# Seven column tiles of a projection taken in 512-column passes, their halves summed by ScalarE and VectorE, with two weight splits and one product moved

## The chip, the cores and the metric

The kernel runs on one NeuronCore of a Trainium2 chip. The metric is the device time of one execution in microseconds (us), the median of several runs.

The profile calls the engines PE (TensorE: matmuls; PEld is its weight load), DVE (VectorE), ACT (ScalarE), POOL (GpSimd) and SP (SyncE, which here only starts DMAs). A line such as L1335 is line 1335 of the kernel before.

## The reference

Three transformer blocks on one sequence of 256 tokens and 2048 features, all in float32. The first two (a pooling mixer and a dilated attention, each with an MLP) are not touched. The third block's mixer projects the normalised tokens once, and splits the result into four parts:

```python
hn = _rmsnorm(h, attn_norm_w[l])
proj = hn @ w_in[l]                       # 2048 -> 1024 + 512 + 256 + 64
u, c_q, c_kv, k_pe = jnp.split(proj, split_at, axis=-1)
y_ssm = _s5_group(u, ...)                 # a scan over the 256 tokens
y_mla = _mla_group(c_q, c_kv, k_pe, ...)  # 8 attention heads
```

`u` drives a diagonal state-space scan. `c_q` (512 columns) and `c_kv` (256) are each RMS-normalised and projected again to the queries, keys and values of eight heads. `k_pe` (64 columns) is a rotary key that all heads share.

## The kernel before

Every matmul weight is a float32 matrix that arrives from HBM in chunks of 128 x 2048 (1 MB; some are narrower). There are four slots. For each chunk SP starts the DMA into `raw` (L525), ACT rounds it into `whi` (`hi1`, L630), and DVE takes the difference `wlo = raw - whi` (`lo1`, L1335); the rounded type runs at full matmul rate. These two steps are called the split of a chunk. A slot of `raw` is loaded anew once its `lo1` is done, in the order of SP's queue; `whi` and `wlo` are free when PE has used the chunk (`chunk_used`). The tokens are held in the same two parts, side by side in `x_pair`: for each of 16 blocks of 128 features, 256 columns of `xhi` and 256 of `xlo`. A product is the sum of three matmuls, as `three` writes them:

```python
pe.matmul(o, w_hi, x_hi, start=first, stop=False)
pe.matmul(o, w_hi, x_lo, start=False, stop=False)
return pe.matmul(o, w_lo, x_hi, start=False, stop=last)
```

The chunks of the mixer have a fixed order, `MIXER`: 0 to 14 are the column tiles of the first projection (tiles 0 to 7 are `u`, 8 to 11 `c_q`, 12 and 13 `c_kv`, 14 `k_pe`), 15 is the value projection `v`, 16 to 18 are heads 0 to 2 (`mla`; 1280 columns wide for even heads, 768 for odd ones), 19 and 20 heads 3 and 4. Each engine works through a list written out by hand, in program order, and waits on counting semaphores.

PE's list in this stretch is: tiles 4 to 6; `drive` 0 and 1 (products that feed the scan of the first half of the state); tiles 7 to 9; `drive` 2 and 3; tiles 10 to 12; `read_out(0)`, which reads the scanned states of the first half; tiles 13 and 14; the sums of squares of the q norm and the kv norm (`norm`, a product with ones); `twin_k`, two products that give the rotary key in both of its forms; `read_out(1)`; and then the heads: `project_q(0)`, `project_v`, `project_k(0)`, `project_q(1)`, scores and so on. A tile of the projection (`proj_tile`, which calls `quad_tile`) takes 16 feature blocks with three matmuls of 256 columns each, and accumulates in one half of a PSUM bank; four tiles share two banks.

ACT's list: splits; `copy_u` (moves `u` out of PSUM); `copy_state` (the driven states); `copy_in(2)` (tiles 8 to 11, 1024 columns in one copy, into `mix_in`), `copy_in(3)` (tiles 12 to 14); the squares of the two norms; `y_copies`, which move the read-out of the first half in 16 pieces; the roots and roundings of the norms; from `copy_q` on the heads, with the v copies (`copy_v_all`) between pieces of the second read-out.

DVE's list: the `lo1` of each chunk between pieces of the scan. The scan of each half has `scan_steps` (`steps_of`), `scan_levels`, and `close_scan` (`scan_carry`, `scan_shift`, and the signal `scan_done`). DVE does 12 of 16 state pairs of a half, POOL the other 4 by a list of its own. After the second half come `wave_k` (multiplies the rotary key by its wave), the q norm, `lo1` of chunk 17, the kv norm, `rope_k` (copies the two products of `twin_k`), pieces of the second read-out, and the heads. `read_out(1)` waits for `scan_done` of the second half, `project_v` for `rope_k` and the kv norm, and the heads for the v copies.

Of the kernel before, what the change touches and what calls it, by code (L numbers as in the profile page):

```python
# [16 lines left out]
ALU = mybir.AluOpType  # L17
ACT = mybir.ActivationFunctionType
AX = mybir.AxisListType

P = 128
T = 256
D = 2048
DT = D // P
# [156 lines left out]
def build(nc, x_t, x_rows, gain_rows, weights, ssm_compact, ssm_skip, features, consts, dist_table, ssm_lam, positions, out):  # L181
    with ExitStack() as ctx:
        def sem(name):
            return ctx.enter_context(nc.semaphore(name))
# [137 lines left out]
        def half(bank, h):  # L322
            return ps[:, bank, h * T:(h + 1) * T]

        def block_ps(b):

            return ps[:, 2 * b:2 * b + 2, :].rearrange("p b (h t) -> p (b h) t", t=T)

        def wait_used(eng, q, s=SLOTS - 1):

            eng.wait_ge(chunk_used, q * SLOTS + (SLOTS + s + 1))
# [12 lines left out]
        def ccol(name, a=0, n=None, rows=P):  # L344
# [37 lines left out]
        angles_ready, trig_ready, table_ready = sem("angles_ready"), sem("trig_ready"), sem("table_ready")  # L382
        drive_done, state_copied, scan_done, scan_rest_done, y_done, y_ready = (
            sem(n) for n in ("drive_done", "state_copied", "scan_done", "scan_rest_done", "y_done", "y_ready"))
        x_tail_free, mla_sq, mla_var, mla_root = sem("x_tail_free"), sem("mla_sq"), sem("mla_var"), sem("mla_root")
        ssm_sq, ssm_var, ssm_root, ssm_high, ssm_low, y_other = (sem(n) for n in ("ssm_sq", "ssm_var", "ssm_root", "ssm_high", "ssm_low", "y_other"))
        gelu_ready, gelu_hi_ready, gelu_lo_ready, glu_sig, gated = (
# [4 lines left out]
                             "m_turned", "m_pt", "m_out", "m_out_copied"))  # L392
        act_steps, dve_steps, pool_steps = sem("act_steps"), sem("dve_steps"), sem("pool_steps")

        source = {"q": [(block_free, 2 + BLOCK["proj"] + 3)], "kv": [(block_free, 2 + BLOCK["proj"] + 4)]}

        def norm_tmp(name):

# [2 lines left out]
        def norm_ps(name):  # L401

            return half({"q": 0, "kv": 1}[name], 0)

        def down_ps(nb):

# [216 lines left out]
        def _(act):  # L623
# [19 lines left out]
            def norm_squares_ahead(name, src):  # L643

                for p in range(PIECES[NORM[name]]):
                    norm_square(name, src, p)

            def norm_root(name):
                k = NORM[name]
                act.wait_ge(norm_lo, LO0[name])  # L650
                act.wait_ge(norm_var, k + 1)
                act.activation(std[:], norm_ps(name), ACT.Sqrt, scale=1.0 / (NORMS[k][1] * P), bias=ccol("rms_eps")).then_inc(norm_std, 1)
# [411 lines left out]
            def hi_mixer(i0, i1):  # L1064
                for c in MIXER[i0:i1]:
                    hi_of(*c)
# [12 lines left out]
                        ins = act.activation(dst, src, ACT.Copy)  # L1079
                ins.then_inc(block_free, 1)  # L1080

            def copy_in(b):
                wait_used(act, *PLACE["proj", 4 * b + 3 if b < 3 else 14])
                n = 4 if b == 2 else 3
                act.activation(mix_in[:, 4 * b - 8:4 * b - 8 + n, :], block_ps(b % 2)[:, 0:n, :], ACT.Copy).then_inc(block_free, 1)

            def copy_state(i):

                act.wait_ge(drive_done, i + 1)
                act.activation(state[:, :, 4 * i:4 * i + 4, ROUND:], ps[:, 4 + i % 4, :].rearrange("p (e r c) -> p r e c", e=4, r=2),  # L1090
                               ACT.Copy).then_inc(state_copied, 1)
# [21 lines left out]
            hi_mixer(12, 14)  # L1113
            for i in range(4, 8):
                copy_state(i)
            hi_mixer(14, 16)
            copy_in(2)
            hi_mixer(16, 18)
            act.wait_ge(x_tail_free, 1)
            y_copies(0, 0, 4, False)  # L1120
            act.wait_ge(x_tail_free, 2)
            norm_squares_ahead("q", mix_in[:, 0:4, :])
            copy_in(3)
            norm_squares_ahead("kv", mix_in[:, 4:6, :])
            norm_root("q")
            hi_mixer(18, 19)
            y_copies(0, 4, 6, False)
# [201 lines left out]
        def _(dve):  # L1329
# [18 lines left out]
            def norm(name, gain, src, dst_hi, dst_lo):  # L1348
                k = NORM[name]
                n, t0 = NORMS[k][1], PIECE0[k]  # L1350
                w = min(4, n)
                y = norm_tmp(name)
                dve.wait_ge(norm_std, k + 1)
                step(dve.reciprocal(rstd[:], std[:]))
                step.settle()

                def lo(p):
                    dve.wait_ge(norm_hi, LO0[name] + p + 1)
                    a = slice(p * w, p * w + w)
                    dve.tensor_tensor(dst_lo[:, a, :], y[:, a, :], dst_hi[:, a, :].bitcast(F32), ALU.subtract).then_inc(norm_lo, 1)  # L1360
                for p in range(PIECES[k]):
                    for i in range(p * w, p * w + w):
                        ins = dve.scalar_tensor_tensor(out=y[:, i, :], in0=src[:, i, :], scalar=fcol(gain, i),
                                                       in1=rstd[:], op0=ALU.mult, op1=ALU.mult)
                    ins.then_inc(norm_y, 1)
                    if p >= 1:
                        lo(p - 1)
                lo(PIECES[k] - 1)
# [608 lines left out]
            def lo_mixer(i0, i1):  # L1977
                for c in MIXER[i0:i1]:
                    lo1(*PLACE[c], mixer_width(*c))

            def steps_of(hf, j0, j1):
                scan_steps(dve, step, scan_tmp, 16 * hf, SCAN_DVE, j0, j1)

            def close_scan(hf):
                for s0 in range(0, SCAN_DVE, 6):
                    scan_carry(dve, step, scan_tmp, 16 * hf + s0, 6)
                scan_shift(dve, step, 16 * hf, SCAN_DVE)
                dve.sem_inc(scan_done, 1)

            def wave_k():  # L1990

                dve.wait_ge(trig_ready, 5)
                dve.wait_ge(block_free, 2 + BLOCK["proj"] + 4)
                dve.tensor_tensor(k_waved[:], mix_in[:, 6, :], rope_wave[:], ALU.mult).then_inc(k_wave_ready, 1)
# [80 lines left out]
            scan_levels(dve, step, scan_tmp, 0, SCAN_DVE)  # L2075
            lo_mixer(12, 13)
            close_scan(0)
            lo_mixer(13, 14)
            dve.wait_ge(state_copied, 7)
            steps_of(1, 1, 3)  # L2080
            lo_mixer(14, 15)
            steps_of(1, 3, 6)
            lo_mixer(15, 16)
            steps_of(1, 6, 8)
            lo_mixer(16, 17)
            scan_levels(dve, step, scan_tmp, 16, SCAN_DVE)
            close_scan(1)
            wave_k()
            norm("q", "mla_q_norm_w_2", mix_in[:, 0:4, :], cq_hi, cq_lo)
            lo_mixer(17, 18)  # L2090
            norm("kv", "mla_kv_norm_w_2", mix_in[:, 4:6, :], ckv_hi, ckv_lo)
            rope_k()
            dve.wait_ge(y_done, 2)
# [317 lines left out]
        def _(pe):  # L2411
# [5 lines left out]
            def chunk(q, s):  # L2417
                pe.wait_ge(lo_ready, q * SLOTS + (SLOTS + s + 1))
# [102 lines left out]
            def quad_tile(q, set_, s, slot, n_used, x_ready=None, order=range(DT), free=False):  # L2521

                chunk(q, slot)
                o = block_ps(set_)[:, s, :]
                for n, k in enumerate(order):
                    if x_ready is not None and n % 4 == 0:
                        pe.wait_ge(x_ready[0], x_ready[1] + n // 4 + 1)
                    c = slice(k * P, k * P + P)
                    ins = three(o, whi[:, s, c], wlo[:, s, c], xhi[:, k, :], xlo[:, k, :], n == 0, n == DT - 1)
                    if free and n in (3, 7):  # L2530
                        ins.then_inc(x_tail_free, 1)
                ins.then_inc(chunk_used, n_used)

            def norm(name, src):
                k = NORM[name]
                n, t0 = NORMS[k][1], PIECE0[k]
                w = min(4, n)
                for p in range(PIECES[k]):
                    pe.wait_ge(norm_sq, t0 + p + 1)
                    for i in range(p * w, p * w + w):  # L2540
                        ins = pe.matmul(norm_ps(name), ones[:], norm_tmp(name)[:, i, :], start=i == 0, stop=i == n - 1)
                ins.then_inc(norm_var, 1)
# [356 lines left out]
            def proj_tile(i):  # L2899
                if i % 4 == 0:  # L2900
                    pe.wait_ge(block_free, n0 + i // 4 + 1)
                q, s = PLACE["proj", i]
                if i == 14:
                    quad_tile(q, i // 4 % 2, i % 4, s, 1, order=LAST_ORDER, free=True)
                else:
                    quad_tile(q, i // 4 % 2, i % 4, s, 1)
            rows_mixed("attn2", QUAD["mixer"], 512, turn_mixer)
            pe.wait_ge(rows_staged, 1)
            proj_tile(4)
# [2 lines left out]
                proj_tile(i)  # L2912
            drive(0)
            drive(1)
            for i in range(7, 10):
                proj_tile(i)
            drive(2)
            drive(3)
            for i in range(10, 13):
                proj_tile(i)  # L2920
            read_out(0)
            for i in range(13, 15):
                proj_tile(i)
            norm("q", mix_in)
            norm("kv", mix_in)
            twin_k()
            read_out(1)

            def project_q(h):

# [329 lines left out]
```

## Time and profile before

| | |
|---|---|
| median of 3 runs | 3127.41 us (3127.34 to 3127.64) |
| profiled execution | 3128.01 us, span 3126.2 us |
| busy share of the span | PE 99%, PEld 83%, DVE 65%, ACT 63%, POOL 14% |
| the stretch from the projection's tile 4 to the first heads | about 2129 to 2262 us of the span |

The span runs from the first to the last instruction of the profile. A busy share is an average over many stages with different limits, and matmuls overlap their neighbours, so PE's 99% is not its peak. Times of rows are counted from the start of the span. In a timeline the start of a matmul is the moment of its issue; the distance from one start to the next is what a matmul costs in a stream, and its own duration, which is longer, is not.

### The profile page before, as it was taken

Reading aid. Unit: us, or ns where it says so; the run is one execution under the profiler, and the core shown is the slowest. Engines: PE = TensorE matmul, PEld = TensorE weight load, DVE = VectorE, ACT = ScalarE, POOL = GpSimd, SP = SyncE. Lnnn points to the kernel's source line nnn. Section 1 sums busy time; section 2 is a strip of 40 time slices with the busy share of each in tenths; the row PEclk is TensorE's granted clock in tenths of the full one; section 3 lists DMA queues with packets and bytes.
Section 4 is the critical chain, followed back from the end, with each engine's and each line's share of the span. In section 5 each row is a group of like instructions: output and inputs, shape, how many; then the busy total and the mean of one; then the engine's idle time right before and its main releaser. Section 6 shows DMA issues by size and latency. Waiting matters only on the chain.

```text
span 3126.2 us, 40499 instructions
## 1 busy us (share of the span) xinstructions
PE 3104.1 (99%) x14653; PEld 2605.3 (83%) x14653; DVE 2032.4 (65%) x1815; ACT 1971.1 (63%) x2737; POOL 447.3 (14%) x562
## 2 busy tenths in 40 slices
PE   9999999999999999999999999999999999999998
PEld 8888888888888888888888888879988888888887
DVE  6876665566565554667655656576876676666767
ACT  7557677666766776666555455556655866666655
POOL 3112443344352000000000000003330000000000
PEclk9999999999999999999999999999999999999999
DMA  8555665565556544546555555536454555545553
GB/s 312 192 201 214 214 211 204 204 218 210 197 174 230 194 176 162 188 162 263 194 189 187 201 190 199 187 136 239 148 190 181 200 190 204 196 175 201 188 203 119
DMA packets 114035, 612.91 MB, mean 196 GB/s; under 512 B 11040, under 2 KB 39840, under 8 KB 43936
## 3 DMA queue, kind: packets, MB, share of 16 engines
q1 hardware_dynamic: 91360, 597.10, 52.1%
q10 hardware_dynamic: 22592, 14.69, 1.5%
q8 instruction: 55, 0.90, 0.1%
q14 instruction: 28, 0.23, 0.0%
HBM read 599.16 MB, written 12.58 MB: 196 GB/s over the span
## 4 chain that ended last, share of the span: by engine, by line
PE 96%; DVE 2%; ACT 1%; issue 0%; DMA 0%; ACTq 0%; DVEq 0%
PE ps L2550 28%; PE ps L2552 28%; PE ps L2551 28%; PE ps L2421 1%; PE ps L2422 1%; PE ps L2423 1%; PE ps L2458 1%; PE ps L2451 1%; PE ps L2445 1%; DVE wlo L1335 1%; PE ps L2623 0%; PE ps L2875 0%; PE ps L2575 0%; PE ps L2777 0%; PE ps L2757 0%; ACT whi L630 0%
## 5 line engine op out<-in xcount | busy, mean ns | idle before, releaser
L1335 DVE TENSOR_TENSOR wlo<-raw,whi 128x2048 fp32r<-128x2048 f32 (+1 forms) x544 | 1245.6, 2300 | 786.1 <-ACT whi L630 782.8
L630 ACT ACTIVATE whi<-raw 128x2048 fp32r<-128x2048 f32 (+1 forms) x544 | 1025.4, 1901 | 853.0 <-PE ps L2552 787.8
L2550 PE MATMUL ps<-whi,x_pair 128*128 128x512 f32 x2400 | 935.9, 390 | 0.0
L2552 PE MATMUL ps<-whi,x_pair 128*128 128x512 f32 x2400 | 933.9, 389 | 0.0
L2551 PE MATMUL ps<-wlo,x_pair 128*128 128x512 f32 x2400 | 933.8, 389 | 0.0
L2552 PEld LDWEIGHTS ps<-whi,x_pair 128*128 128x128 f32 x2400 | 450.5, 188 | 93.8
L2551 PEld LDWEIGHTS ps<-wlo,x_pair 128*128 128x128 f32 x2400 | 450.6, 188 | 93.3
L2550 PEld LDWEIGHTS ps<-whi,x_pair 128*128 128x128 f32 x2400 | 450.6, 188 | 93.1
L2550 PE MATMUL ps<-whi,hid_hi 128*128 128x512 f32 x1280 | 499.3, 390 | 0.0
L2551 PE MATMUL ps<-wlo,hid_hi 128*128 128x512 f32 x1280 | 498.0, 389 | 0.0
L2552 PE MATMUL ps<-whi,hid_lo 128*128 128x512 f32 x1280 | 498.0, 389 | 0.0
L2552 PEld LDWEIGHTS ps<-whi,hid_lo 128*128 128x128 f32 x1280 | 240.3, 188 | 49.9
L2550 PEld LDWEIGHTS ps<-whi,hid_hi 128*128 128x128 f32 x1280 | 240.4, 188 | 49.8 <-issue 0.4
L2551 PEld LDWEIGHTS ps<-wlo,hid_hi 128*128 128x128 f32 x1280 | 240.4, 188 | 49.3
L1373 DVE TENSOR_TENSOR resid<-resid,ps 128x1024 f32<-128x1024 f32 x165 | 200.7, 1217 | 105.3 <-PE ps L2552 104.9
L702 ACT ACTIVATE hid<-up_turns 32x256 f32<-32x256 f32 x512 | 213.0, 416 | 6.1 <-DVE up_turns L1509 0.5
L452 POOL TENSOR_TENSOR scan_room<-state,hop 128x64 f32<-128x64 f32 (+3 forms) x20 | 10.0, 500 | 1199.2 <-ACT state L1090 1197.7
L2178 DVE SCALAR_TENSOR_TENSOR conv<-up_sum,feat,conv 128x255 f32<-128x255 f32 (+1 forms) x176 | 73.3, 479 | 85.7 <-ACT conv L1278 83.0
L927 ACT ACTIVATE qk_t<-qk_turns 32x256 f32<-32x256 f32 x192 | 80.0, 417 | 48.5 <-DVE qk_turns L1840 46.4
L2335 POOL TENSOR_TENSOR job_tmp<-compact,z_pow 128x128 f32<-128x128 f32 x32 | 70.9, 2215 | 85.2 <-DVEq L1783 82.3
L702 ACT ACTIVATE up_sum<-value_turns 32x256 f32<-32x256 f32 x176 | 73.4, 417 | 5.4 <-DVE value_turns L1509 3.5
L759 ACT ACTIVATE drive_out<-drive_turns 32x128 f32<-32x128 f32 x240 | 74.3, 310 | 3.0
(410 smaller groups left out, 3096.2 us busy)
## 6 DMA issues: line engine op xcount, KB each, us to landing
raw<-weights SPq DMA_DIRECT2D x536, 1024.0 KB, 4.8
read_tab<-read_tables SPq DMA_DIRECT2D x2, 3072.0 KB, 11.5
read_tables<-c_wide ACTq DMA_DIRECT2D x32, 128.0 KB, 1.9
drive_tables<-drive_out ACTq DMA_DIRECT2D x16, 256.0 KB, 3.7
drive_tab<-drive_tables SPq DMA_DIRECT2D x4, 1024.0 KB, 9.5
raw<-weights SPq DMA_DIRECT2D x6, 512.0 KB, 9.7
raw<-weights SPq DMA_DIRECT2D x4, 640.0 KB, 12.1
resid<-x_rows SPq DMA_DIRECT2D x1, 2048.0 KB, 13.0
```

Of the source, the lines that this page charges most:

```text
L630: act.activation(whi[:, s, 0:width], raw[:, s, 0:width], ACT.Copy).then_inc(hi_ready, 1)
L702: ins = act.activation(to, src, func)
L759: ins = act.activation(drive_out[32 * k:32 * k + 32, :, :, 32 * i:32 * i + 32].rearrange("p e r c -> p (e r) c"), drive_turns[32 * i:32 * ...
L927: ins = act.activation(to, part, ACT.Copy)
L1335: dve.tensor_tensor(wlo[:, s, 0:width], raw[:, s, 0:width], whi[:, s, 0:width].bitcast(F32), ALU.subtract).then_inc(lo_ready, 1)
L1373: return dve.tensor_tensor(r, r, ps[:, bank:bank + 2, :], ALU.add).then_inc(sem_, n)
L2178: ins = dve.scalar_tensor_tensor(out=o, in0=up_sum[:, half_, nt, 0:T - lag], scalar=fcol("ffn_conv_w_2", i + tap * (2 * FF2 // P)), in1=o, ...
L2335: step(pool.tensor_tensor(a, src.unsqueeze(2).to_broadcast(shape), straight, ALU.mult))
L2421: pe.matmul(o, w_hi, x_hi, start=first, stop=False)
L2550: pe.matmul(o, xh[:, k, t], whi[:, s, c], start=first and j == 0, stop=False)
L2551: pe.matmul(o, xh[:, k, t], wlo[:, s, c], start=False, stop=False)
L2552: ins = pe.matmul(o, xl[:, k, t], whi[:, s, c], start=False, stop=last and j == 3)
```

## The change

The seven tiles 8 to 14 are taken by a new function, `pair_tile`. For each feature block it has two matmuls instead of three: `whi` with the whole of `x_pair`, 512 columns, which fills a whole bank (high product in the first half, `whi` times `xlo` in the second), and `wlo` with `xhi`, 256 columns, accumulated in the first half. Each tile has a bank to itself: tiles 8 to 11 banks 0 to 3, tile 12 bank 0, tile 13 bank 2, tile 14 bank 3.

The two halves are summed by two engines: ACT copies the first half to `mix_in` (`copy_pair`, seven copies instead of two), and DVE adds the second half from PSUM to it (`pair_sum`). DVE's seven additions stand between the pieces of the scan; that of tile 13 stands ahead of `scan_levels` of the second half, that of tile 14 ahead of `wave_k`. DVE's splits (`lo1`) of chunks 15 and 16 move from between the `steps_of` of the second half to behind `wave_k` and behind the q norm. PE's `twin_k` moves from ahead of `read_out(1)` to behind it. Other waits follow the new banks.

```diff
@@ -382,6 +382,7 @@
         angles_ready, trig_ready, table_ready = sem("angles_ready"), sem("trig_ready"), sem("table_ready")
         drive_done, state_copied, scan_done, scan_rest_done, y_done, y_ready = (
             sem(n) for n in ("drive_done", "state_copied", "scan_done", "scan_rest_done", "y_done", "y_ready"))
+        pair_copied, pair_summed = sem("pair_copied"), sem("pair_summed")
         x_tail_free, mla_sq, mla_var, mla_root = sem("x_tail_free"), sem("mla_sq"), sem("mla_var"), sem("mla_root")
         ssm_sq, ssm_var, ssm_root, ssm_high, ssm_low, y_other = (sem(n) for n in ("ssm_sq", "ssm_var", "ssm_root", "ssm_high", "ssm_low", "y_other"))
         gelu_ready, gelu_hi_ready, gelu_lo_ready, glu_sig, gated = (
@@ -392,7 +393,7 @@
                              "m_turned", "m_pt", "m_out", "m_out_copied"))
         act_steps, dve_steps, pool_steps = sem("act_steps"), sem("dve_steps"), sem("pool_steps")
 
-        source = {"q": [(block_free, 2 + BLOCK["proj"] + 3)], "kv": [(block_free, 2 + BLOCK["proj"] + 4)]}
+        source = {"q": [(block_free, 2 + BLOCK["proj"] + 3)], "kv": [(pair_summed, 5)]}
 
         def norm_tmp(name):
 
@@ -401,6 +402,10 @@
         def norm_ps(name):
 
             return half({"q": 0, "kv": 1}[name], 0)
+
+        def pair_bank(i):
+
+            return {12: 0, 13: 2, 14: 3}.get(i, i % 4)
 
         def down_ps(nb):
 
@@ -1079,10 +1084,10 @@
                         ins = act.activation(dst, src, ACT.Copy)
                 ins.then_inc(block_free, 1)
 
-            def copy_in(b):
-                wait_used(act, *PLACE["proj", 4 * b + 3 if b < 3 else 14])
-                n = 4 if b == 2 else 3
-                act.activation(mix_in[:, 4 * b - 8:4 * b - 8 + n, :], block_ps(b % 2)[:, 0:n, :], ACT.Copy).then_inc(block_free, 1)
+            def copy_pair(i):
+
+                wait_used(act, *PLACE["proj", i])
+                act.activation(mix_in[:, i - 8, :], half(pair_bank(i), 0), ACT.Copy).then_inc(pair_copied, 1)
 
             def copy_state(i):
 
@@ -1113,15 +1118,18 @@
             hi_mixer(12, 14)
             for i in range(4, 8):
                 copy_state(i)
+            for i in range(8, 12):
+                copy_pair(i)
             hi_mixer(14, 16)
-            copy_in(2)
+            copy_pair(12)
             hi_mixer(16, 18)
+            copy_pair(13)
             act.wait_ge(x_tail_free, 1)
             y_copies(0, 0, 4, False)
             act.wait_ge(x_tail_free, 2)
             norm_squares_ahead("q", mix_in[:, 0:4, :])
-            copy_in(3)
             norm_squares_ahead("kv", mix_in[:, 4:6, :])
+            copy_pair(14)
             norm_root("q")
             hi_mixer(18, 19)
             y_copies(0, 4, 6, False)
@@ -1987,6 +1995,12 @@
                 scan_shift(dve, step, 16 * hf, SCAN_DVE)
                 dve.sem_inc(scan_done, 1)
 
+            def pair_sum(i):
+
+                dve.wait_ge(pair_copied, i - 7)
+                y = mix_in[:, i - 8, :]
+                dve.tensor_tensor(y, y, half(pair_bank(i), 1), ALU.add).then_inc(block_free if i in (11, 14) else pair_summed, 1)
+
             def wave_k():
 
                 dve.wait_ge(trig_ready, 5)
@@ -2075,19 +2089,25 @@
             scan_levels(dve, step, scan_tmp, 0, SCAN_DVE)
             lo_mixer(12, 13)
             close_scan(0)
+            pair_sum(8)
+            pair_sum(9)
             lo_mixer(13, 14)
             dve.wait_ge(state_copied, 7)
             steps_of(1, 1, 3)
             lo_mixer(14, 15)
+            pair_sum(10)
+            pair_sum(11)
             steps_of(1, 3, 6)
-            lo_mixer(15, 16)
+            pair_sum(12)
             steps_of(1, 6, 8)
-            lo_mixer(16, 17)
+            pair_sum(13)
             scan_levels(dve, step, scan_tmp, 16, SCAN_DVE)
             close_scan(1)
+            pair_sum(14)
             wave_k()
+            lo_mixer(15, 16)
             norm("q", "mla_q_norm_w_2", mix_in[:, 0:4, :], cq_hi, cq_lo)
-            lo_mixer(17, 18)
+            lo_mixer(16, 18)
             norm("kv", "mla_kv_norm_w_2", mix_in[:, 4:6, :], ckv_hi, ckv_lo)
             rope_k()
             dve.wait_ge(y_done, 2)
@@ -2531,6 +2551,25 @@
                         ins.then_inc(x_tail_free, 1)
                 ins.then_inc(chunk_used, n_used)
 
+            def pair_tile(i, order=range(DT)):
+
+                q, s = PLACE["proj", i]
+                if i == 14:
+                    pe.wait_ge(block_free, BLOCK["proj"] + 5)
+                elif i >= 12:
+                    pe.wait_ge(pair_summed, 2 * i - 23)
+                else:
+                    pe.wait_ge(block_free, BLOCK["proj"] + (3 if i < 10 else 4))
+                chunk(q, s)
+                bank, r = pair_bank(i), i % 4
+                for n, k in enumerate(order):
+                    c = slice(k * P, k * P + P)
+                    pe.matmul(ps[:, bank, :], whi[:, r, c], x_pair[:, k].rearrange("p h t -> p (h t)"), start=n == 0, stop=False)
+                    ins = pe.matmul(half(bank, 0), wlo[:, r, c], xhi[:, k, :], start=False, stop=n == DT - 1)
+                    if i == 14 and n in (3, 7):
+                        ins.then_inc(x_tail_free, 1)
+                ins.then_inc(chunk_used, 1)
+
             def norm(name, src):
                 k = NORM[name]
                 n, t0 = NORMS[k][1], PIECE0[k]
@@ -2900,10 +2939,7 @@
                 if i % 4 == 0:
                     pe.wait_ge(block_free, n0 + i // 4 + 1)
                 q, s = PLACE["proj", i]
-                if i == 14:
-                    quad_tile(q, i // 4 % 2, i % 4, s, 1, order=LAST_ORDER, free=True)
-                else:
-                    quad_tile(q, i // 4 % 2, i % 4, s, 1)
+                quad_tile(q, i // 4 % 2, i % 4, s, 1)
             rows_mixed("attn2", QUAD["mixer"], 512, turn_mixer)
             pe.wait_ge(rows_staged, 1)
             proj_tile(4)
@@ -2912,19 +2948,21 @@
                 proj_tile(i)
             drive(0)
             drive(1)
-            for i in range(7, 10):
-                proj_tile(i)
+            proj_tile(7)
+            for i in range(8, 10):
+                pair_tile(i)
             drive(2)
             drive(3)
             for i in range(10, 13):
-                proj_tile(i)
+                pair_tile(i)
             read_out(0)
-            for i in range(13, 15):
-                proj_tile(i)
+            pair_tile(13)
+            pair_tile(14, LAST_ORDER)
+            pe.wait_ge(pair_summed, 4)
             norm("q", mix_in)
             norm("kv", mix_in)
+            read_out(1)
             twin_k()
-            read_out(1)
 
             def project_q(h):
```

## Rows read from the trace of the kernel before

**Rows 1.** The page's chain of work that ended last, by engine.
```profile
PE 96%; DVE 2%; ACT 1%; issue 0%; DMA 0%; ACTq 0%; DVEq 0%
```

**Rows 2.** PE's waits, 2125 to 2420 us: total, times, longest.
```profile
PE ps L2550 <- DVE ssm_lo L2041: 0.9, 1, 0.9
```

**Rows 3.** PE's timeline: start, us, instruction, count [idle before <-releaser]; matmuls of two widths.
```profile
2127.59 1.98 PE L2498 MATMUL ps<-wlo,x_pair 128*128 128x512 f32 x8
2129.40 0.28 PE L2421 MATMUL ps<-x_pair,whi 128*128 128x256 f32 x1
2129.52 0.28 PE L2422 MATMUL ps<-x_pair,whi 128*128 128x256 f32 x1
```

**Rows 4.** PE's timeline, the first rows of five blocks.
```profile
2196.38 0.33 PE L2888 MATMUL ps<-u_step,read_tab 128*128 128x64 f32 x2
...
2207.02 0.36 PE L2421 MATMUL ps<-x_pair,whi 128*128 128x256 f32 x1
...
2221.30 0.59 PE L2896 MATMUL ps<-k_waved,const 128*128 128x256 f32 x2
...
2222.17 0.33 PE L2888 MATMUL ps<-u_step,read_tab 128*128 128x64 f32 x2
...
2235.76 0.40 PE L2960 MATMUL ps<-whi,ckv_hi 128*128 128x512 f32 x1
```

**Rows 5.** ACT's timeline, 2213 to 2242 us.
```profile
2213.11 0.85 ACT L630 ACTIVATE whi<-raw 128x768 fp32r<-128x768 f32 x1 [15.20 <-PE ps L2423]
...
2230.60 0.63 ACT L661 ACTIVATE ckv_hi<-kv_tmp 128x512 fp32r<-128x512 f32 x1
...
2235.96 0.39 ACT L1138 ACTIVATE m_io<-ps 128x256 f32<-128x256 f32 x1 [0.44 <-PE ps L2423]
...
2237.34 0.60 ACT L1149 ACTIVATE v_all<-ps 128x512 f32<-128x512 f32 x1 [0.31 <-PE ps L2962]
...
2241.42 0.60 ACT L1149 ACTIVATE v_all<-ps 128x512 f32<-128x512 f32 x1 [0.18 <-PE ps L2962]
```

**Rows 6.** DVE's timeline, 2200 to 2233 us.
```profile
2200.16 2.29 DVE L1335 TENSOR_TENSOR wlo<-raw,whi 128x2048 fp32r<-128x2048 f32 x1
...
2205.50 1.49 DVE L1335 TENSOR_TENSOR wlo<-raw,whi 128x1280 fp32r<-128x1280 f32 x1
2206.91 0.37 DVE L452 TENSOR_TENSOR scan_room<-state,hop 128x168 f32<-128x168 f32 x1
...
2211.51 0.61 DVE L483 TENSOR_TENSOR scan_room<-pow_re,state 128x294 f32<-128x294 f32 x1
...
2216.00 0.47 DVE L483 TENSOR_TENSOR scan_room<-pow_re,state 128x294 f32<-128x294 f32 x1
...
2219.79 0.22 DVE L498 COPY state<-state 128x168 f32<-128x168 f32 x1
...
2220.22 0.43 DVE L1994 TENSOR_TENSOR k_waved<-mix_in,rope_wave 128x256 f32<-128x256 f32 x1 [0.21 <-DVE state L498]
2221.10 1.75 DVE L1354 RECIPROCAL rstd<-std 128x256 f32<-128x256 f32 x1 [0.46 <-ACT std L652]
...
2227.70 1.75 DVE L1354 RECIPROCAL rstd<-std 128x256 f32<-128x256 f32 x1
2229.48 0.88 DVE L1363 SCALAR_TENSOR_TENSOR kv_tmp<-mix_in,feat,rstd 128x256 f32<-128x256 f32 x2
...
2231.87 0.68 DVE L1999 COPY k_rope<-ps 128x512 f32<-128x512 f32 x1
```

**Rows 7.** POOL's timeline, the last row of its scan.
```profile
2215.75 0.30 POOL L498 COPY state<-state 128x56 f32<-128x56 f32 x1
```

**Rows 8.** The page's DMA issues: count, KB each, us to landing.
```profile
raw<-weights SPq DMA_DIRECT2D x4, 640.0 KB, 12.1
```

**Rows 9.** Windows: us, busy of PE, PEld, DVE, ACT, POOL; PEclk, DMA share, GB/s.
```profile
111.00:114.30 3.30, 0.33 (x3) 0.14 (x3) 3.21 (x5) 0.05 (x1) 1.81 (x4) 1.00 0.59 199
114.90:118.30 3.40, 3.40 (x19) 3.40 (x18) 2.38 (x2) 2.21 (x2) 0.00 (x0) 0.50 0.59 248
```

## The prediction

> **What bounds the kernel now.** I read the page first, for the bound. The chain of work that ended last is 96% TensorE (PE); VectorE (DVE) and ScalarE (ACT) hold 3% [rows 1]. Whatever shortens PE's own work shortens the end, and whatever makes PE wait lengthens it. The change touches one stretch, so I next read PE's waits over 2125 to 2420 us, from the first projection tile to the output products: the longest entry is 0.9 us [rows 2]. There is hardly a wait here to win back. Then I read PE's timeline for the price of a matmul and the order of the blocks, ACT's and DVE's timelines for who has slack, POOL's for what runs beside DVE, and the granted clock.
>
> PE's order in the stretch is a chain without a hole: the first read-out from 2196.38, tiles 13 and 14 from 2207.02, the norm sums, the twin product from 2221.30, the second read-out from 2222.17, then the q product, the v product from 2235.76 [rows 4]. The second read-out needs DVE's scan, behind whose last piece `wave_k` starts at 2220.22 [rows 6]: about 2 us before PE arrives. That is all the slack that the scan has.
>
> **The matmuls.** Eight matmuls of 512 columns take from 2127.59 to 2129.40, 0.226 each; one of 256 columns is followed by the next after 0.12 [rows 3]. A tile is now 16 x 3 x 0.12 = 5.76 us and becomes 16 x (0.226 + 0.12) = 5.54. Seven tiles: PE saves 7 x 0.22 = 1.5 us, 0.05% of the time. That is the whole direct gain. No row alternates the two widths inside one bank. Where the width changes at 2129.40, nothing is added [rows 3], so I take 0.346 a step; as the other end a step keeps its 0.36 and the 1.5 us are not gained.
>
> The Trainium skill ("TensorE: Matmul & The Clock Gate", Back-to-back issue gap) gives a matmul its columns at the clock and a fixed 2.5 ns more; by that, dropping one matmul in three saves 16 x 7 x 2.5 ns = 0.3 us, an estimate. The rows show a larger part that does not grow with the columns (2 x 0.12 - 0.226 = 14 ns), and they decide.
>
> **The sums.** Before, two ACT copies took seven column blocks; now seven copies of 256 columns at 0.39 (the `m_io` copy from PSUM has that shape) [rows 5], and DVE gets seven additions of 128x256 with one operand in PSUM. No row has that form: 128x256 without PSUM is 0.43, a 128x512 copy from PSUM 0.68 [rows 6]. I take 0.43, whose shape is the same; the end above adds 0.25 to each, the end below is ACT's 0.39. The ACT copies themselves cost nothing: ACT stands idle 15.2 us before 2213.11 [rows 5]. The copy of tile 11 now stands ahead of the split of chunk 14 and holds it until tile 11 is done, near 2190; DVE comes to that chunk near 2194 and PE near 2212, so it is covered. Tiles 12, 13 and 14 wait for the sums of tiles 8, 10 and 11 to free their banks. By the same steps these end near 2188, 2197 and 2197, and the tiles begin near 2189.5, 2206 and 2211: covered, the first by 1.5 us, and a later sum would cost what it exceeds that by.
>
> **The new wait, and where it stands.** DVE works in program order. The sum of tile 13 stands before `scan_levels` of the second half, so the last part of the scan is queued behind tile 13. And PE runs tile 13 only after the first read-out. Before, ACT's split of chunk 17, released by the end of tile 13, starts at 2213.11 [rows 5]. Six tiles (8 to 13) are 0.22 shorter each: 2211.8. ACT first does that split (0.85), then the copy (0.39): 2213.05. With the sum: 2213.5. DVE gets there earlier: it began the split of chunk 16 at 2205.50; without the split of chunk 15 (2.29) [rows 6] and with five sums (2.15) that is 2205.4. So DVE stands idle some 7.7 us, with the rest of the scan, `wave_k`, both norms and the rope behind it.
>
> From 2206.91 (levels) to 2220.22 (`wave_k`) DVE needs 13.3 us [rows 6]. POOL ran its share beside it until 2216.05 [rows 7]. Of the sixteen carry operations the first eight took 4.49 (2211.51 to 2216.00), the next eight 3.79 (to 2219.79) [rows 6]. POOL does not wait for tile 13, and while DVE idles it has no company; it should be done when DVE resumes. So I take the later rate for all: levels 4.60 x 3.79 / 4.49 = 3.9, carry 7.6, rest 0.4, together 11.9 (bound above: the old 13.3; below: 11.2, if the levels gain twice as much). `wave_k` or what stands in its place comes at 2225.4 instead of 2220.22, and the scan's signal some 0.2 before. PE, with 1.5 us saved and the twin product (0.87) moved behind, arrives near 2222.17 - 2.4 = 2219.8 and waits 5.4 us.
>
> **What is late next.** The reciprocal of the q norm began at 2221.10. Now the sum of tile 14 (0.43), `wave_k` (0.43) and the moved split of chunk 15 (2.29) come first: 2228.5. The q norm and chunk 17's split take 6.6 (to 2227.70), chunk 16's moved split 1.4 (2205.50 to 2206.91): 2236.5, where the trace has 2227.70 [rows 6]. DVE is 8.8 us late, and with it the kv norm, `rope_k` (ends 2241.35 instead of 2231.87 + 0.68) and the copies behind it.
>
> PE's side of this: 2225.2, the read-out 10.6 (as 2196.38 to 2207.02), the twin products 0.9, the q product 3.0 (from 2232.8 to 2235.76) [rows 4]: 2239.7. Then it waits for the rope until 2241.35. Moving the twin product therefore costs nothing: DVE covers it by 1.6 us. Without that cover it would cost its own 0.9.
>
> ACT took `ckv_hi` at 2230.60; its input was there at 2229.48 + 0.88 = 2230.36 [rows 5, 6], but ACT was still copying. Now ACT waits for it until 2239.15, so ACT is 8.55 late. It gets back its three waits for PE that follow, 0.44 + 0.31 + 0.18 [rows 5], since the v product is only 5.6 us late. The last v copy, for which PE waits, is 8.55 - 0.93 = 7.6 us late. From there heads, softmax and the glu products pass from ACT to DVE to PE, with PE's holes under 1 us each [rows 2], so nothing gives the 7.6 us back.
>
> The moved splits issue no DMA, but free their raw slots 26 and 29 us later, and SP's queue, in order, holds chunks 19, 20 and all after them until then. Chunk 19 is asked for at 2228.5, chunk 20 near 2235.6; 640 KB take 12.1 us to land (median) [rows 8], so they are in by 2247.7. ACT turns to chunk 19 only after the last v copy (2241.42 + 0.60 [rows 5], now + 7.6: 2249.6). Hidden, by 2 us for the later chunk at the least; without that cover ACT would wait for the difference.
>
> **The sum.** PE's saved 1.5 us is spent inside the wait. Profiled execution 3128.0 (span 3126.2 and 1.8 around it) + 7.6 = 3135.6; the median of the runs is 0.6 under that execution, so 3135.0. With the scan at 13.3 it is 3136.4, with dearer sums on the path (13 and 14) 3136.9, with no gain on the tiles 1.3 more, 3138.2; with the scan at 11.2, 3134.3. About 0.2%, 6.3 us, can be told from no change here.
>
> **The clock.** After the one hole like the new one, 3 us at 111 us, the granted clock is 0.50, the lower level (1.2 GHz), for 3.4 us [rows 9]. A hole of 5.4 us should do the same in the read-out: up to 1.7 us lost there, twice that if two such stretches follow. PE has 1.6 us to spare at the rope, and its v products are 2 us ahead of ACT's copies, so I count nothing. The Trainium skill has it so too ("TensorE: Matmul & The Clock Gate", Why this matters for your kernels): a longer pause of PE between bursts puts the array at half clock. Here the trace agrees, 0.50 at 114.9 us; if none of it were hidden the sum would be 1.7 us more.
>
> **The rivals.** First, the loss is partly absorbed (no change by 0.2%): the scan alone on DVE, or the copies after it, run 1.4 us or more quicker than I sum, or ACT catches up in its gaps. For it: the margin over 6.3 us is only 1.3. Against it: PE's holes after 2240 are too small to take up a delay. About 3132.5. Second, on the other side, the wait does not bind: the sum of tile 13 is ready when DVE arrives at 2205.4. It decides from a sum done by about 2207. Then the scan ends by 2219, PE does not stall, chunk 16's 1.4 us and the sums lengthen the norm chain, and the 1.5 us from PE pays for them: 3127 to 3129. Against it: 10.6 us of read-out stand between tiles 12 and 13 [rows 4]. No row gives more than 1.5 us, so a gain over 0.2% needs an error elsewhere. Third, it is worse: the clock's loss is not hidden, or alternating the widths costs; 0.04 us a step more over six tiles is 3.8 us, all on the path: 3137.5 to 3140.
>
> **Chances.** As summed, 3133.8 to 3137.5: 0.6. Absorbed: 0.2. Wait not binding: 0.07. Worse: 0.13. The range 3130.0 to 3138.5 leaves out the second rival and the end of the third. Slower: 0.73; same 0.25; faster 0.02.
>
> **What would show it.** Right: DVE idle 7 to 8 us before the sum of tile 13, released by ACT; PE idle about 5 us at the first matmul of the second read-out, released by DVE; `rope_k` near 2241 and the v product behind it; tiles of 5.5 us; a clock row of 0.50 near 2226. Wrong: PE without a hole there, tiles other than 5.5 us, or PE's later blocks shifted by clearly less than the v copies.

## The result, and the profile after

The changed kernel takes 3144.45 us (median of 6 runs, 3143.48 to 3144.84), the kernel before 3127.91 beside it (6 runs): a ratio of 1.0053, 95% interval 1.0042 to 1.0063. It is slower by 16.5 us; the forecast was slower by 7.6, and the result lies above its range. The profiled execution is 3144.51 us, its span 3142.7.

The page's chain of work that ended last, by engine, is what it was [rows 1]:

```profile
PE 96%; DVE 2%; ACT 1%; issue 0%; DMA 0%; ACTq 0%; DVEq 0%
```

The page's shares don't show a loss of 0.5%. The view of PE's waits, 2125 to 2440 us (total, times, longest), does; its second row is the old longest one [rows 2]:

```profile
PE ps L2927 <- issue: 5.0, 1, 5.0
PE ps L2589 <- DVE ssm_lo L2055: 0.9, 1, 0.9
```

PE's timeline (start, us, instruction, count, idle before): first a piece of a pair tile, then the blocks [rows 3, 4]:

```profile
2160.71 0.40 PE L2567 MATMUL ps<-x_pair,whi 128*128 128x512 f32 x1
2160.94 0.28 PE L2568 MATMUL ps<-x_pair,wlo 128*128 128x256 f32 x1
2161.06 0.40 PE L2567 MATMUL ps<-x_pair,whi 128*128 128x512 f32 x1
...
2225.86 0.66 PE L2927 MATMUL ps<-u_step,read_tab 128*128 128x64 f32 x2 [4.96 <-issue]
...
2246.36 1.17 PE L2935 MATMUL ps<-k_waved,const 128*128 128x256 f32 x2
...
2247.82 0.78 PE L2441 MATMUL ps<-cq_hi,whi 128*128 128x256 f32 x1
...
2251.43 0.40 PE L2998 MATMUL ps<-whi,ckv_hi 128*128 128x512 f32 x1
```

The hole is there, 4.96 us, ahead of the second read-out. The row names no releaser; DVE's scan ends at 2225.70, 0.16 us before the read-out starts. But the read-out then lasts from 2225.86 to the twin product at 2246.36, 20.5 us where the first one took 10.6 [rows 4]. The v product starts 15.67 us later than before (2251.43 against 2235.76), and the hole is a third of that. The two executions do not reach the stretch at the same time, though. PE's first row of `drive` 0, which stands ahead of all that the change touches, in the kernel before and in the changed one:

```profile
2147.54 7.26 PE L2875 MATMUL ps<-u_step,drive_tab 128*128 128x64 f32 x64
2147.81 7.26 PE L2914 MATMUL ps<-u_step,drive_tab 128*128 128x64 f32 x64
```

So 0.27 us of that are none of the change's; counted from this row, the v product is 15.4 us late. Below, "from the drive" means counted in this way.

The windows (us, busy of PE, PEld, DVE, ACT, POOL; granted clock, DMA share, GB/s) say why [rows 9]:

```profile
2220.00:2226.00 6.00, 1.04 (x6) 0.61 (x5) 5.51 (x15) 2.85 (x4) 0.00 (x0) 0.93 0.00 0
2226.00:2230.00 4.00, 4.00 (x20) 4.00 (x20) 3.90 (x4) 0.00 (x0) 0.00 (x0) 0.50 0.01 2
2230.00:2240.00 10.00, 10.00 (x49) 10.00 (x48) 8.37 (x11) 6.26 (x10) 0.00 (x0) 0.50 0.36 115
2240.00:2249.00 9.00, 9.00 (x39) 8.64 (x39) 1.27 (x2) 4.41 (x6) 0.00 (x0) 0.50 0.26 107
2249.00:2260.00 11.00, 11.00 (x70) 9.84 (x69) 10.62 (x26) 7.54 (x18) 0.00 (x0) 1.00 0.00 1
```

The mean of 0.93 in the first row means that the clock fell to its lower level (0.50, 1.2 GHz) about 0.8 us before 2226, while PE stood. It came back only at 2249: 23.9 us, in the last 23.2 of which PE never stood. After the old hole it was low for 3.4 us [rows 9]. There, in the kernel before, products of 256 columns follow the hole:

```profile
114.31 0.35 PE L2421 MATMUL ps<-pool_hi,whi 128*128 128x256 f32 x1 [2.99 <-issue]
```

DVE's timeline (start, us, instruction, idle before and its releaser) [rows 6]:

```profile
2213.97 0.42 DVE L2002 TENSOR_TENSOR mix_in<-mix_in,ps 128x256 f32<-128x256 f32 x1 [8.93 <-ACT mix_in L1090]
2214.31 0.33 DVE L457 TENSOR_TENSOR scan_room<-state,hop 128x168 f32<-128x168 f32 x1
...
2225.48 0.22 DVE L503 COPY state<-state 128x168 f32<-128x168 f32 x1
...
2228.92 1.75 DVE L1362 RECIPROCAL rstd<-std 128x256 f32<-128x256 f32 x1
...
2236.91 1.75 DVE L1362 RECIPROCAL rstd<-std 128x256 f32<-128x256 f32 x1
...
2248.42 0.69 DVE L2013 COPY k_rope<-ps 128x512 f32<-128x512 f32 x1 [7.46 <-PE ps L2936]
```

The sum of tile 13 waits 8.93 us, and the scan and both norms follow it as forecast. The last row is not as forecast: DVE is ready for the rope at 2240.95 and waits 7.46 us for PE, where PE should have waited for DVE.

ACT's timeline, the copies behind the slow read-out and the last v copy [rows 5]:

```profile
2251.63 0.38 ACT L1146 ACTIVATE m_io<-ps 128x256 f32<-128x256 f32 x1 [7.14 <-PE ps L2443]
...
2257.10 0.60 ACT L1157 ACTIVATE v_all<-ps 128x512 f32<-128x512 f32 x1 [0.19 <-PE ps L3000]
```

The last v copy, for which the heads wait, is 15.68 us late (2241.42 before), 15.4 from the drive. From there on the delay stays what it is: the last rows of DVE's output are 15.6 us late as well. The other 0.9 of the 16.5 us by which the span is longer lie behind these rows: the span ends 5.8 us after they begin, and 4.9 before.

### The profile page after: what moved, and what is told of

It is laid out like the page before. It is cut to its first block, busy times and chain, and to the rows that moved or that the text cites. A ratio compares the mean times of both kernels' runs of the same rounds, so it can differ in the third digit from the quotient of the medians.

```text
span 3142.7 us, 40293 instructions
## 1 busy us (share of the span) xinstructions
PE 3116.0 (99%) x14541; PEld 2611.1 (83%) x14541; DVE 2033.2 (65%) x1822; ACT 1967.5 (63%) x2742; POOL 440.8 (14%) x562
## 4 chain that ended last, share of the span: by engine, by line
PE 96%; DVE 2%; ACT 1%; issue 0%; DMA 0%; ACTq 0%; DVEq 0%
PE ps L2589 28%; PE ps L2591 28%; PE ps L2590 28%; PE ps L2478 1%; PE ps L2567 1%; PE ps L2441 1%; PE ps L2471 1%; PE ps L2442 1%; PE ps L2443 1%; PE ps L2465 1%; DVE wlo L1343 1%; PE ps L2662 0%; PE ps L2914 0%; PE ps L2568 0%; PE ps L2614 0%
```

## The experiments

Theory A: the wait for tile 13 makes the scan late, PE gets a hole, and the hole costs twice, once as delay and once through a clock that stays low over the whole read-out. B: the read-out is slow by itself, from the new tiles or banks. C: the moved splits of chunks 15 and 16 make the norms late, and that is the loss. Ratios are to the kernel before on the same chip, with 95% intervals.

**The wait taken away.** The sum of tile 13 moves into the middle of the scan, which then doesn't wait for tile 13; all else is the changed kernel.

```diff
-            pair_sum(13)
             scan_levels(dve, step, scan_tmp, 16, SCAN_DVE)
-            close_scan(1)
+            scan_carry(dve, step, scan_tmp, 16, 6)
+            pair_sum(13)
+            scan_carry(dve, step, scan_tmp, 22, 6)
+            scan_shift(dve, step, 16, SCAN_DVE)
+            dve.sem_inc(scan_done, 1)
```

> Undoes the new wait alone: the sum of tile 13 stands between the two halves of scan_carry instead of ahead of scan_levels; all else is the changed kernel. Theory A (DVE's wait for tile 13 makes a hole of 5 us on PE, and the hole lowers the clock for the read-out): no wait of DVE over 1 us, scan done by about 2219, no hole, the read-out in 10.6 us, 3127 to 3129 us. Rival B (the read-out is slow because of something that the paired tiles bring): still 20 us for the read-out, 3137 or more. Rival C (the splits moved behind the scan make the norms late): about 3.7 us of the loss stay, 3131 to 3132.

Measured: 3129.16 us, ratio 1.0004 (0.9995 to 1.0013). Its window over most of the read-out, its DVE timeline, PE's rows (the drive, the read-out's start, the twin product behind it, the v product), and ACT's last v copy:

```profile
2222.00:2233.00 11.00, 11.00 (x95) 10.90 (x95) 9.11 (x14) 7.80 (x12) 0.00 (x0) 1.00 0.43 152
```

```profile
2212.53 0.42 DVE L2002 TENSOR_TENSOR mix_in<-mix_in,ps 128x256 f32<-128x256 f32 x1
...
2216.64 0.22 DVE L503 COPY state<-state 128x168 f32<-128x168 f32 x1
...
2232.34 0.68 DVE L2013 COPY k_rope<-ps 128x512 f32<-128x512 f32 x1
```

```profile
2146.36 7.26 PE L2917 MATMUL ps<-u_step,drive_tab 128*128 128x64 f32 x64
...
2219.28 0.33 PE L2930 MATMUL ps<-u_step,read_tab 128*128 128x64 f32 x2
...
2229.95 0.65 PE L2938 MATMUL ps<-k_waved,const 128*128 128x256 f32 x2
...
2233.73 0.40 PE L3001 MATMUL ps<-whi,ckv_hi 128*128 128x512 f32 x1
```

```profile
2241.05 0.60 ACT L1157 ACTIVATE v_all<-ps 128x512 f32<-128x512 f32 x1
```

No idle time before the sum, the scan done at 2216.9, no hole, the clock at 1.00, the read-out done in 10.7 us. The pair tiles and the moved splits are all in it, so neither B nor C holds. It gains nothing either: from the drive, its v product starts 0.85 us earlier than before, but the last v copy is 0.8 us later.

**The hole filled.** The changed kernel, with 22 products of 512 columns (chunk 15's rounded weights with themselves) while PE would stand, into a bank that the read-out overwrites afterwards; the late scan stays.

```diff
+            def dense(n):
+
+                q, s = PLACE["v", 0]
+                pe.wait_ge(hi_ready, q * SLOTS + (s + 1))
+                for _ in range(n):
+                    pe.matmul(ps[:, 7, :], whi[:, s, 0:P], whi[:, s, 0:512], start=True, stop=True)
...
             norm("kv", mix_in)
+            dense(22)
             read_out(1)
```

> The changed kernel, with 22 products of 512 columns added on PE between the kv norm and the second read-out (chunk 15 with itself, into a bank that the read-out then overwrites; they take 5.0 us and their result is not used). They fill the hole; DVE's wait for tile 13 stays. Theory A: clock 1.00 throughout, the read-out in 10.6 instead of 20.5 us, rope_k near 2241, and only the loss of the late scan is left: 3135 to 3137. Rival B: the read-out still takes about 20 us, 3144 to 3145.

Measured: 3136.69 us, ratio 1.0027 (1.0016 to 1.0037). PE's waits, its drive, and ACT's last v copy:

```profile
PE ps L2441 <- ACT v_all L1157: 2.0, 1, 2.0
PE ps L3006 <- DVE k_rope L2013: 1.2, 1, 1.2
```

```profile
2147.02 7.25 PE L2914 MATMUL ps<-u_step,drive_tab 128*128 128x64 f32 x64
```

```profile
2248.71 0.60 ACT L1157 ACTIVATE v_all<-ps 128x512 f32<-128x512 f32 x1
```

The clock stays at 1.00 and the read-out takes 10.7 us. Now PE waits for the rope, as forecast for the change itself. The last v copy is at 2248.71, from the drive 7.8 us later than before: that is the late scan alone. In the changed kernel it is 7.6 us later still: that is the clock.

**The wait alone.** The kernel before, with one line more and nothing else of the change.

```diff
             lo_mixer(16, 17)
+            wait_used(dve, *PLACE["proj", 13])
             scan_levels(dve, step, scan_tmp, 16, SCAN_DVE)
```

> The kernel before with one wait added: DVE waits for the end of tile 13 ahead of scan_levels of the second half. No paired tiles, no sums, no moved splits, no moved twin product. Theory A: scan done near 2225, a hole of 4 to 5 us on PE ahead of the twin product, the clock at 0.50 through the read-out, 3141 to 3144. Rival B: the hole costs its own length and the read-out keeps 10.6 us, 3132 to 3134.

Measured: 3144.78 us, ratio 1.0054 (1.004 to 1.0067), just above what A expected. PE's timeline and a window:

```profile
2226.11 1.22 PE L2897 MATMUL ps<-k_waved,const 128*128 128x256 f32 x2 [4.03 <-DVE k_waved L1994]
```

```profile
2226.00:2249.00 23.00, 22.89 (x103) 22.54 (x104) 9.71 (x15) 10.65 (x15) 0.00 (x0) 0.50 0.13 46
```

This one wait alone costs as much as the whole change, and the change without it costs nothing that can be told. Here the two twin products, 256 columns wide, still stand ahead of the read-out; they did not raise the clock, which stayed low for 27.3 us, to 2253.2.

**The splits back in their places.** The changed kernel with the splits of chunks 15 and 16 between the scan's steps again.

```diff
             pair_sum(12)
+            lo_mixer(15, 16)
             steps_of(1, 6, 8)
+            lo_mixer(16, 17)
             pair_sum(13)
...
             wave_k()
-            lo_mixer(15, 16)
             norm("q", ...)
-            lo_mixer(16, 18)
+            lo_mixer(17, 18)
```

> The changed kernel with the splits of chunks 15 and 16 back at their old places, ahead of the sum of tile 13, in DVE's idle time. Theory A: DVE stands ready 7.5 us before the twin product ends, so what it saves (3.7 us) is on no path: 3144 to 3145, as the changed kernel. Rival C: the moved splits are part of the loss, 3140 to 3141.

Measured: 3144.73 us, ratio 1.0054 (1.004 to 1.0068); a hole of 5.1 us, the clock low for 23.9 us. The norms come earlier, and DVE only waits longer for PE ahead of the rope: 10.90 us instead of 7.46. C is out.

**What follows the hole.** The hole stays, and 16 useless products (`dense`, as above) of 512 columns stand behind it, ahead of the read-out. Theory A2: what PE runs behind the hole decides how long the clock stays low. Theory D: it stays low for its time, whatever PE runs.

```diff
             norm("kv", mix_in)
+            pe.wait_ge(scan_done, 2)
+            dense(16)
             read_out(1)
```

> The changed kernel with the hole kept: PE waits for the scan as before, then does 16 products of 512 columns (chunk 15 with itself, result not used), then the read-out. Theory A2 (what comes after the hole decides how long the clock stays low: the read-out's products of 64 columns do not bring it back, products of 256 or 512 columns do): the 16 products take 4 to 7 us, part of them at 0.43 each, the clock returns during them, the read-out takes 10.6 us: 3139 to 3141. Rival D (the clock stays low for some 24 us whatever is done): 6.8 us for the products and 20 for the read-out, 3150 to 3152.

Measured: 3139.13 us, ratio 1.0036 (1.0024 to 1.0049). PE's timeline and three windows:

```profile
2224.59 6.33 PE L2943 MATMUL ps<-whi 128*128 128x512 f32 x16 [4.92 <-DVEq L1996]
2230.75 0.33 PE L2927 MATMUL ps<-u_step,read_tab 128*128 128x64 f32 x2
```

```profile
2225.00:2229.00 4.00, 4.00 (x10) 3.05 (x10) 3.90 (x4) 0.00 (x0) 0.00 (x0) 0.50 0.04 11
2229.00:2231.00 2.00, 2.00 (x10) 1.66 (x9) 1.97 (x5) 0.00 (x0) 0.00 (x0) 0.81 0.57 175
2234.00:2242.00 8.00, 8.00 (x71) 7.95 (x71) 5.00 (x6) 6.68 (x11) 0.00 (x0) 1.00 0.59 209
```

The same hole (its releaser, L1996, is the line that signals `scan_done`), and the clock is low for only 6.8 us: by the mean of 0.81 in the second window it is back near 2229.8, while the wide products run. The read-out then runs at full rate, 2230.75 to 2241.4. Six us of useless work on the path make the changed kernel 5.3 us faster. A2 holds, D does not. What it is in these products that raised the clock is not shown: they differ from the read-out's passes in width, in the number format (rounded weights, against plain float32 in two passes) and, from the two twin products of the wait alone, also in how long they run.

**Half of the hole filled.** 11 dense products ahead of the read-out instead of 22, so that 2.45 us of hole remain.

```diff
             norm("kv", mix_in)
+            dense(11)
             read_out(1)
```

> The changed kernel with 11 instead of 22 products of 512 columns ahead of the wait for the scan: a hole of about 2.5 us is left. If a hole of 2.5 us leaves the clock alone, as the holes of up to 1.7 us near 2104 us do in the kernel before: 3136 to 3137, the read-out in 10.6 us. If it lowers the clock, as the one of 3 us at 111 us does: 3144 to 3145.

Measured: 3142.59 us, ratio 1.0039 (1.0026 to 1.0051). Neither expectation holds for all: four of the six executions took 3142.46 to 3143.31, with a mean granted clock of 0.995, the other two 3135.64 and 3136.90, with 0.999. The profiled one is of the first kind; its windows:

```profile
2224.00:2227.00 3.00, 1.04 (x10) 1.07 (x10) 2.62 (x9) 0.00 (x0) 0.00 (x0) 1.00 0.00 0
2227.00:2240.00 13.00, 13.00 (x71) 13.00 (x70) 11.47 (x12) 6.17 (x10) 0.00 (x0) 0.56 0.27 83
```

By the mean of 0.56 the clock fell near 2228.6, some 2.7 us after PE had begun the read-out at 2225.96 and with PE busy, and it stayed low for 20.5 us. So this hole sometimes costs the clock and sometimes not. What decides between the two in one execution stays open.

**The hole filled with thin products.** 23 products of 64 columns, of the read-out's own form, instead of the wide ones.

```diff
+            def thin(n):
+
+                pe.wait_ge(read_landed, 32)
+                for _ in range(n):
+                    pe.matmul(ps[:, 7, 0:64], read_tab[:, 0, 2, :], u_step[:, 16, :], start=True, stop=True)
...
             norm("kv", mix_in)
+            thin(23)
             read_out(1)
```

> The changed kernel with 23 products of the read-out's own form (64 columns, two passes each, 0.22 us; result not used) in the hole instead of products of 512 columns. If work of any width holds a high clock (the drives and the first read-out, 7 to 10.6 us of such products, run at 1.00): 3136 to 3137. If such thin products count as a pause: clock 0.50 by the read-out, 3144 to 3145.

Measured: 3137.02 us, ratio 1.0028 (1.0017 to 1.004). The windows over the fill and over the read-out:

```profile
2219.00:2225.00 6.00, 6.00 (x48) 5.74 (x46) 5.66 (x14) 2.87 (x5) 0.00 (x0) 1.00 0.00 0
2225.00:2236.00 11.00, 11.00 (x101) 11.00 (x99) 9.49 (x14) 3.25 (x5) 0.00 (x0) 1.00 0.12 37
```

Thin products in the hole keep the high clock as well as wide ones do. Yet thin products of the same form did not bring it back in the changed kernel.

## Why the prediction was wrong, by its steps

**The step that failed is the price of the clock.** The prediction saw that the hole would lower the clock, took the 3.4 us of the only like hole in the trace, doubled it at most, set the loss against 1.6 us that PE has to spare at the rope, and wrote "so I count nothing". The clock stayed low for 23.9 us. Against the kernel with the hole filled, the read-out takes 20.5 us instead of 10.7, the twin product 1.46 instead of 0.73, and the q product 0.4 more. The 1.2 us that PE waits for the rope there, and the 2.1 us by which the last v copy follows the start of the v product more closely in the changed kernel (5.7 us instead of 7.8), take some of that back. What is left is 7.6 us at the last v copy, against the forecast's worst case of 1.7 to 3.4. The error was to carry a duration over from a place where other work followed: behind the old hole stood products of 256 columns, but the second read-out is a run of 64-column passes, and nothing wide comes behind it until the twin and the q product. The third rival named this cause ("the clock's loss is not hidden"), but priced it, with the dearer tiles, at 3137.5 to 3140.

**The late scan was right, place and size.** DVE's idle time ahead of the sum was 8.93 us (forecast 7.7), the scan behind it 11.5 (11.9), with POOL done with its share by 2212.1; PE's hole 4.96 (5.4), and the filled hole puts the last v copy 7.8 us late from the drive (7.6). The wait alone is enough for it, as the kernel before with one more line shows. In whole times the filled hole reads 8.4 us. Here the prediction lacks a term: in the profiled executions of the changed kernel and of all kernels built on it the span ends 5.7 to 5.8 us after DVE's last row begins, in the kernel before and in the wait alone 4.9. What lengthens this tail stays open. So the 16.5 us are about 7.8 for the late scan, 7.6 for the clock, 0.9 for the tail and 0.3 from ahead of the drive.

**The tile was sized too well.** A step of a pair tile takes 0.35 us (0.23 + 0.12), not 0.346 exactly: three tiles run from 2179.08 to 2196.12, 5.68 each instead of 5.54. The same three took 5.79 each before (2179.02 to 2196.38), so a tile saves 0.11 us. Seven save 0.7, not 1.5: from the drive, the sums of squares behind them start 0.74 us earlier. In the changed kernel that is spent in the hole anyway.

**The sums were right.** 0.42 us each (0.43), with one operand in PSUM; ACT's copies 0.37 to 0.38 (0.39).

**The twin product's cover did not hold.** It was to cost nothing since DVE would still be busy with the norms. DVE was ready 7.46 us before PE, so the twin, 1.46 us at the low clock, stood on PE's path. Where the hole is filled, PE waits for the rope and the cover is there.

**The norms and loads were right.** The reciprocals began at 2228.92 and 2236.91 (2228.5, 2236.5). Among ACT's waits between 2205 and 2290 us there is none for a transfer, so the raw slots that come free later cost nothing; and with the splits put back the time is the same.

**The rivals.** "The wait does not bind" fails by the 8.93 us. "Partly absorbed" fails too: nothing gave the delay back. No row spoke for a gain above 1.5 us, and with the wait gone the kernel is level with the one before: the tiles' 0.7 us are less than can be told, and ACT's copies, not PE, set the last v copy there.

## What to carry to other kernels

Before an instruction is put into an engine's list, ask what stands behind it: here one small addition held a scan for which PE had 2 us to spare. A hole in TensorE's stream is priced not only by its own length, but also by what PE runs behind it at the lower clock; a low stretch read elsewhere in the trace holds only for the work that followed it there. If a hole can't be avoided, fill it, even with products that nobody reads, or try wide products ahead of a run of thin ones: here 16 useless ones behind the hole gained 5.3 us, while two of 256 columns did not raise the clock. Two profiled executions can be shifted against each other ahead of the change (here by up to 1.8 us), so count times from a row that the change does not touch before you subtract them.

## What the runs showed of the hardware

With PE busy in all but the first 0.7 us at most, the granted clock stayed at 0.50 for 23.9 us (the changed kernel), 27.3 (the wait alone) and 20.5 (half filled), as long as 64-column passes ran. It rose once 256-column products had followed them for a while: 2.7 us after the first of these in the changed kernel, 2.0 with the splits back, 4.9 in the wait alone, 5.1 half filled. With 16 products of 512 columns behind the same hole it rose after 6.8 us. At the lower clock a read-out pass took 0.21 us (20.5 over 96), at the higher one 0.11 (11.0 over 101). Thin passes kept the clock high where it was high already.

The Trainium skill ("TensorE: Matmul & The Clock Gate", What's actually happening) has it that the slow stretch at the start of work is a matter of time, and not of how many matmuls are issued. Behind a hole the runs differ, and they decide: what is issued matters too. Behind holes of 4.92 and 4.96 us, the low stretch was 6.8 us with wide products and 23.9 with thin ones, of which 5.2 and 23.2 lie behind the end of the hole. Why the thin ones do not raise the clock was not taken further.
